# The sample's tile joins the last prompt batch in a fused attention and expert-retrieval kernel

## The reference

```python
h = rmsnorm(x, g_norm1); z = h @ w_in
x = x + concat[GLA(z_gla), FoX(z_fox)] @ w_out
h2 = rmsnorm(x, g_norm2)
q = (h2 @ w_q).reshape(blk, 8, 2, 128)
s = einsum('nhcd,hckd->nhck', q, subkeys)
s1, i1 = top_k(s[:, :, 0], 16); s2, i2 = top_k(s[:, :, 1], 16)
top, ti = top_k(s1[..., :, None] + s2[..., None, :], 16)
idx = i1[ti // 16] * 128 + i2[ti % 16]
coeff = softmax(top) * gelu(einsum('nhkd,nd->nhk', u_tab[idx], h2))
x = x + einsum('nhk,nhkd->nd', coeff, v_tab[idx])
```

## Time and profile before

| | |
|---|---|
| three runs | 3724.64, 3728.86, 3737.84 us, median 3728.86 |
| profiled execution | 3727.01 us, its span 3725.2 us |
| busy share of the span | PE 76%, DVE 71%, ACT 40%, POOL 35% |
| mean granted TensorE clock | 0.881 |
| gathers | 1056 issues; their queue moved 1131.10 MB |
| all DMA | 1268.10 MB, mean 340 GB/s |

### The profile page before, as it was taken

The page is one execution under the profiler, slowest core; times in us unless marked ns, Lnnn a source line. Parts: engine busy times, 40 slices in busy tenths (PEclk is TensorE's granted clock), DMA queues, the critical chain, the costliest instruction groups (busy, mean ns, idle before and its releaser), DMA issues.

```text
span 3725.2 us, 32330 instructions
## 1 busy us (share of the span) xinstructions
PE 2838.7 (76%) x8403; PEld 1468.9 (39%) x8403; DVE 2658.0 (71%) x5553; ACT 1479.7 (40%) x3869; POOL 1316.1 (35%) x1145
## 2 busy tenths in 40 slices
PE   7998998667777877677777677777877777687677
PEld 3454444543333343333334333333343333243333
DVE  5344334278688777899687798777777887887786
ACT  2333333135345633344543344444533443343344
POOL 0000000034444444444344434434444453444443
PEclk9999998788888888898889888878888898888889
DMA  4001000699999999999999999999999999999998
GB/s 190 23 23 46 23 23 22 263 360 417 411 417 399 419 419 419 375 403 402 415 420 420 420 407 419 355 400 400 420 420 419 413 411 406 410 404 414 420 418 350
DMA packets 187373, 1268.10 MB, mean 340 GB/s; under 512 B 23380, under 2 KB 24492, under 8 KB 39860
## 3 DMA queue, kind: packets, MB, share of 16 engines
q0 software_dynamic: 159488, 1131.10, 74.4%
q1 hardware_dynamic: 25348, 122.22, 8.2%
q10 hardware_dynamic: 2352, 12.72, 0.8%
HBM read 1239.08 MB, written 26.88 MB: 340 GB/s over the span
## 4 chain that ended last, share of the span: by engine, by line
DMA 33%; PE 21%; DVE 14%; issue 8%; ACT 4%; POOL 2%; SPq 0%; DVEq 0%; ACTq 0%; POOLq 0%
DMA uv_ring<-in_peer_uv,expert_index 32%; PE ps_acc L1458 14%; DVE uv_ring L1634 6%; PE ps_scores L1433 3%; DVE v_sums L1642 2%; POOL uv_ring L1098 2%; PE ps_scores L1314 1%; ACT coef_diag L1271 1%; PE ps_scores L1401 1%; ACT gelu_u_dot_h L1266 1%; DVE key_top_index L1544 1%; DVE key_scores_rest L1545 1%; PE ps_turn L1325 1%; DVE key_top_index L1553 1%; PE ps_fox_o L1332 1%
## 5 line engine op out<-in xcount | busy, mean ns | idle before, releaser
L1458 PE MATMUL ps_acc<-uv_ring,coef_diag 128*128 128x512 f32 x2676 | 1530.6, 714 | 743.2 <-ACT coef_diag L1271 725.8
L1098 POOL DMA_INDIRECT uv_ring<-in_peer_uv,expert_index x1056 | 1268.5, 1201 | 1661.8 <-PE ps_acc L1458 1467.8
L1634 DVE CUSTOM_DVE_ANT_0 uv_ring<-uv_ring,h_rows 128x1024 f32<-128x1024 f32 x1056 | 1286.5, 1221 | 460.0 <-DMA uv_ring<-in_peer_uv,expert_index 438.0
L1458 PEld LDWEIGHTS ps_acc<-uv_ring,coef_diag 128*128 128x128 f32 x2676 | 556.7, 222 | 1525.1 <-ACT coef_diag L1271 995.1
L1266 ACT ACTIVATE gelu_u_dot_h<-u_dot_h 128x2 f32<-128x2 f32 x528 | 107.1, 203 | 1317.1 <-DVE u_dot_h L1634 1315.2
L1642 DVE SCALAR_TENSOR_TENSOR v_sums<-uv_ring,coefficients,v_sums 128x1024 f32<-128x1024 f32 x387 | 496.2, 1282 | 10.5 <-ACT coefficients L1273 9.5
L392 PE MATMUL ps_z<-w_in,x_T 128*128 128x512 f32 x864 | 416.3, 630 | 5.7 <-DVE w_in L677 5.7
L1433 PE MATMUL ps_scores<-weight_chunk,rows_T 128*128 128x256 f32 x1152 | 261.9, 381 | 0.7 <-issue 0.7
L1271 ACT ACTIVATE coef_diag<-coef_diag,gelu_u_dot_h 128x128 f32<-128x128 f32 x669 | 253.1, 398 | 17.7
L1433 PEld LDWEIGHTS ps_scores<-weight_chunk,rows_T 128*128 128x128 f32 x1152 | 220.4, 192 | 62.5 <-issue 35.8
L392 PEld LDWEIGHTS ps_z<-w_in,x_T 128*128 128x128 f32 x864 | 164.8, 200 | 193.5 <-issue 181.3
(11 more groups left out here) (205 smaller groups left out, 2582.5 us busy)
## 6 DMA issues: line engine op xcount, KB each, us to landing
weight_chunk<-scratch_keys_w SPq DMA_DIRECT2D x48, 1024.0 KB
weight_chunk<-in_w_out_chunks SPq DMA_DIRECT2D x24, 1024.0 KB
uv_ring<-in_peer_uv,expert_index POOLq DMA_INDIRECT x1056
w_in<-in_w_in_chunks SPq DMA_DIRECT2D x6, 2048.0 KB, 25.4
uv_ring<-in_w_peer_q_T SPq DMA_DIRECT2D x8, 1024.0 KB, 24.9
x_T<-in_x_T POOLq DMA_DIRECT2D x9, 512.0 KB, 4.6
x_rows<-in_x_rows POOLq DMA_DIRECT2D x9, 512.0 KB, 5.3
x_mid<-in_x_rows SPq DMA_DIRECT2D x9, 512.0 KB, 15.9
```

Source lines behind the costliest of these rows:

```text
L1098: pool.indirect_dma_start(out=ring[:, s % RING, :], out_offset=None, in_=dram["uv"], in_offset=bass.IndirectOffsetOnAxis(ap=idx[:, t % IDX ...
L1458: mm = pe.matmul(acc[:, c, :], diag[:, r, :], ring[:, r, D + c * 512:D + (c + 1) * 512], start=first, stop=False, skip_group_check=True)
L1634: dve.tensor_tensor_reduce(out=ring[:, s % RING, 0:D], in0=ring[:, s % RING, 0:D], in1=h2[:, t % 2, :], scale=1.0, scalar=0.0, op0=ALU.mul ...
```

## The change

The sample's tile becomes the third of the last batch. Room for a third `x_mid` and `rows_T` comes from dropping both copies of `match_replace` (it now writes in place) and one buffer of `h2_rows`. With one buffer, h2 is remade at the first slot of a tile, after all dots of the tile before. Every second head of folded keys is staged in `k_pairs_T` in four pieces of 512 floats, and both stores name four pieces.

```diff
-BATCHES = [[0], [1], [2, 3], [4, 5], [6, 7], [8]]
+BATCHES = [[0], [1], [2, 3], [4, 5], [6, 7, 8]]
...
+def mix_free(t):
+    return (mix_fill(t) if PLACE[t + 2][0] == PLACE[t][0] else h2_fill(t)) + 2
...
-    s2 = sb("key_scores_rest", [P, 2, NKEY])
-    cand2 = sb("candidates_rest", [P, TOPK, TOPK])
-    h2 = sb("h2_rows", [P, 2, D])
+    h2 = sb("h2_rows", [P, D])
-    folded = [sums[:].rearrange("p b n -> p (b n)"), h2[:].rearrange("p b n -> p (b n)")]
+    folded = [sums[:].rearrange("p b (c n) -> p (b c) n", c=2), kT[:, :, P:P + 512]]
...
             if t >= 2:
-                sp.wait_ge(q_t, h2_fill(t - 2) + 2)
+                sp.wait_ge(q_t, mix_free(t - 2))
...
-                for n in range(2):
-                    pool.wait_ge(f_st[n], 16 * (PH // 2))
+                pool.wait_ge(f_st[0], 16 * (PH // 2))
...
-        act.wait_ge(init, 2)
+        act.wait_ge(init, 1)
...
+                    if t == 1:
+                        act.wait_ge(f_st[1], 16 * (PH // 2))
...
-            act.dma_start(dram["keys_w"][h], folded[h % 2]).then_inc(f_st[h % 2], 16)
+            act.dma_start(dram["keys_w"][h].rearrange("p (c n) -> p c n", c=4), folded[h % 2]).then_inc(f_st[h % 2], 16)
...
                     act.wait_ge(q_t, mix_fill(t) + 2)
+                    if i >= 2:
+                        act.wait_ge(q_t, h2_fill(t - 2) + 2)
...
-        dve.memset(cand2[:], 0.0).then_inc(init, 1)
...
-                        dve.wait_ge(q_t, h2_fill(t - 2) + 2)
+                        dve.wait_ge(q_t, mix_free(t - 2))
...
-                    did(dve.match_replace(out=rest(c), in_to_replace=v(c)[:, 0:8], in_values=values(c), imm_value=NEG_FILL))
+                    did(dve.match_replace(out=values(c), in_to_replace=v(c)[:, 0:8], in_values=values(c), imm_value=NEG_FILL))
...
-                if i == SLOTS - 4 and t < TILES:
-                    reopen(t + 1)
+                if i == 0 and 0 < t <= TILES:
+                    dve.wait_ge(dotted, SLOTS * t)
+                    reopen(t)
```

More of the change, by code:

```diff
@@ L1474, in fold_out @@
                 dve.wait_ge(f_st[h % 2], 16 * (h // 2))
-            dve.tensor_copy(folded[h % 2][:, part * 512:(part + 1) * 512], acc[:, u % 2, :]).then_inc(f_ev, 1)
+            dve.tensor_copy(folded[h % 2][:, part, :], acc[:, u % 2, :]).then_inc(f_ev, 1)
         def attend(t):
@@ L1535, in did, with top16 @@
                 return ins.then_inc(chain, 1)
-            def top16(values, rest, v, i, count):
+            def top16(values, v, i, count):
                 for c in range(count):
@@ L1548, in top16 @@
                 for c in range(count):
-                    did(dve.max(out=v(c)[:, 8:16], in_=rest(c)))
+                    did(dve.max(out=v(c)[:, 8:16], in_=values(c)))
                 yield
@@ L1552, in top16 @@
                 for c in range(count):
-                    ins = dve.max_index(out=i(c)[:, 8:16], in_max=v(c)[:, 8:16], in_values=rest(c))
+                    ins = dve.max_index(out=i(c)[:, 8:16], in_max=v(c)[:, 8:16], in_values=values(c))
                     if c < count - 1:
@@ L1560, in router @@
             wait(dve, kf_r, n)
-            ins = yield from top16(lambda c: keys[:, c, :], lambda c: s2[:, c, :], lambda c: kv[:, c, :], lambda c: ki[:, c, :], 2)
+            ins = yield from top16(lambda c: keys[:, c, :], lambda c: kv[:, c, :], lambda c: ki[:, c, :], 2)
             ins.then_inc(k_in, 1)
@@ L1570, in router @@
             flat = cand[:].rearrange("p a b -> p (a b)")
-            flat2 = cand2[:].rearrange("p a b -> p (a b)")
             wait(dve, tex, n)
-            ins = yield from top16(lambda c: flat, lambda c: flat2, lambda c: tv[:], lambda c: ti[:], 1)
+            ins = yield from top16(lambda c: flat, lambda c: tv[:], lambda c: ti[:], 1)
             ins.then_inc(top_r, 1)
@@ L1616, in reopen @@
             dve.wait_ge(p_rs, t + 1)
-            dve.scalar_tensor_tensor(out=h2[:, b, :], in0=sums[:, b, :], scalar=hrs[:, t:t + 1], in1=g2[:],
+            dve.scalar_tensor_tensor(out=h2[:], in0=sums[:, b, :], scalar=hrs[:, t:t + 1], in1=g2[:],
                                      op0=ALU.mult, op1=ALU.mult).then_inc(h_r, 1)
@@ L1633, in back @@
                         wait(dve, geld, g - 1)
-                    dve.tensor_tensor_reduce(out=ring[:, s % RING, 0:D], in0=ring[:, s % RING, 0:D], in1=h2[:, t % 2, :], scale=1.0, scalar=0.0,
+                    dve.tensor_tensor_reduce(out=ring[:, s % RING, 0:D], in0=ring[:, s % RING, 0:D], in1=h2[:], scale=1.0, scalar=0.0,
                                              op0=ALU.mult, op1=ALU.add, accum_out=dots[:, g % 2, n:n + 1]).then_inc(dotted, 1)
```

## The result

The changed kernel takes 3819.01 us (median of 4, 3814.15 to 3825.19) against 3730.5 in the same comparison: a ratio of 1.0232, 95% interval 1.0212 to 1.0252. It is slower, as forecast, but by 88 us where 27 were forecast, and outside the range of 3706 to 3802. Its profiled execution took 3817.34 us, its span is 3815.4.

A forecast was written before the change was run, and what follows sets the result against it. Transfers bound attention, projection and the last slots; VectorE's work plus its wait for scores bound routing of pairs. Terms summed to 3751 us of span, 3753 of time, plus 3 for waits: 3756, range 3706 to 3802.

The forecast's parts named there:

- Rival (a): Transfers bind in routing too, so fewer bytes win: 3712 us, or 3697 if only the bytes move; chance 0.25.
- Rival (b): At tile 8's attention TensorE waits for the past's keys and values, costing 10 to 30 us: 3775; chance 0.13.
- Rival (c): More badly placed routing units than counted, 7 us each, five more making 3790; chance inside the forecast's own 0.62.
- bad units: Routing units where VectorE waits about 8.3 us for key scores; 1, 2 and 2 counted in the last three batches.
- 3 us of margin: Added to the summed time because the wait for scores rises with VectorE's load, a third step up.
- Step 1: Start up to slot 0: 787 us, unchanged; stores in 2 KB pieces might cost 12 in all, taken as 0.
- 2, attention and projection: 446 slots where transfers bind, 507.1 MB at the old mean rate: 1223 us, denser work covered by idle engine time.
- Step 3: Routing of tile 0 in 110 us; of tile 1 in 153, 131 busy plus 22 idle as before.
- 4, pairs: Routing of tiles 2 and 3, and 4 and 5: 262 us busy, 26 and 33 waits, 5 idle: 293 and 300.
- 5, last batch: Routing of tiles 6, 7 and 8 up to slot 868: 356 us busy, 40 waits, 7 other: 403.
- 6, the rest: Last 187 slots, nearly pure transfers at 420 GB/s: 473 us, plus 9.4 from last dot to end: 482.
- The position: TensorE's step in ScalarE's copy slot behind adds, VectorE's one slot later, group ahead all TensorE's: 8.3 us wait.

The follow-up runs named there:

- shift of the steps: Changed kernel with VectorE's steps of a unit, and the ScalarE steps that follow, two front steps later: 3717.91 us; one front step later: 3760.49 us.
- density run: Kernel before, own batches and all 72 chunk loads, every due slot of the plan multiplied by 0.875: 3788.32 us, ratio 1.0153.
- old-batches run: Changed kernel with the old list of batches, so only its small edits and no shared pass: 3739.62 us, ratio 1.002.
- contiguous store: Changed kernel with every second head of folded keys staged in 8192 contiguous bytes of unused row buffers: 3814.85 us in a single execution.
- all repairs: Changed kernel with VectorE's steps two front steps later, folded keys in 8192-byte pieces and no adds on VectorE beside routing: 3689.59 us, ratio 0.989.

## Why the prediction was right in kind and wrong in size

Right: the kernel has two regimes; routing of pairs is set by VectorE and its wait for scores, not by transfers; the new plan makes all that precedes slot 868 denser and leaves the end to the transfers; the result is slower. The shift of the steps showed the wait and the density run the plan. Rival (a), transfers bind in routing, fell with both: VectorE waited 4.0 us for data in 311. Rival (b), the wait for the past, did not appear: in the stretch of the last attention TensorE waited for nothing but diagonals and probabilities. Rival (c), more bad units than counted, held for one unit, below.

The sum of 3751 us of span, before its 3 us of margin, was 64 short of 3815.4. By its own steps:

| step | forecast | measured |
|---|---|---|
| 1, up to slot 0 | 787 | 798.2 |
| 2, attention and projection | 1223 | 1226.9 |
| 3, routing of tile 0, of 1 | 110, 153 | 108.5, 161.6 |
| 4, pairs | 293, 300 | 310.8, 310.7 |
| 5, last batch | 403 | 413.2 |
| 6, the rest | 482 | 476.1 + 9.4 |

**Steps 3 to 5 failed by 46 us.** VectorE's time in them, split into its work, its wait for scores and its other idle time:

| stretch | forecast | measured |
|---|---|---|
| routing of 1 | 131 + 22 of idle | 131.0 + 22.0 + 8.6 |
| of 2 and 3 | 262 + 26 + 5 | 266.6 + 34.6 + 9.6 |
| of 4 and 5 | 262 + 33 + 5 | 266.6 + 32.4 + 11.7 |
| of the last batch | 356 + 40 + 7 | 358.7 + 43.0 + 11.5 |

The wait for scores is the largest part, some 25 us, and 14 of them stand where no unit was counted at all. Step 3 carried tile 1's idle time of before over, 22 us, of which 7.7 was wait for scores; the new plan made that wait 22.0. In the other three batches the wait was 11 us too low: the five units that the prediction counted (slots 242, 466, 478, 782, 794) waited 9.1, 7.9, 3.9, 8.9 and 4.1 us, not 8.3 each, one that it did not count waited 6.4 (slot 266), and all 49 uncounted ones had a mean of 1.6 and not 1.2. That the wait of tiles 4 and 5 came out right, 32.4 against 33, is luck: one of its two bad units was priced at twice its wait, and the others too low. VectorE's work was 12 us too low: a slot less took (285.0 - 266.6) / 14 = 1.31 us off its busy time with tiles 2 and 3, not 1.62, and why stays open. Other idle time was some 10 too low.

The position was defined too narrowly. Taken unit by unit from plan and trace, what matters is whether VectorE's step comes one slot after TensorE's or two. Before, 13 units stood one slot apart and waited 2.7 us each, 56 stood two apart and waited 0.7. The new plan puts 31 one slot apart, at 3.3 us, and 36 two apart, at 0.9. With tile 1 it is 6 of 8 units, where it was 3. With VectorE's steps one front step later only 6 units in all stand one slot apart, with two steps later none.

**Step 1 failed by 11 us**: the text bounded the stores in 2 KB pieces by 12 and took 0. The old-batches run put it at 8 for all small edits, the contiguous store at some 7 for the pieces.

**The range failed** since its upper end held the wait only as more units of 8 us and took the start as free. Besides, 0.25 of the chance lay on rival (a), whose own test, the 5 to 11 us of wait for data in the earlier trace rows, already spoke against it. The Trainium skill, Perfetto Trace Analysis, section Identifying the Most-Contended Engine, says to optimize the engine used most. Taken as the prediction took it for (a), that rule would have promised 3697 to 3712 here; the measured 3819 goes against it. The same page's section Optimization Strategy says that interleaving regimes may help, and the trace agrees: the last 187 slots, left nearly alone, had VectorE busy 62% beside full transfers, while routing from tile 1 to slot 868, packed denser, ran at only 363 to 382 GB/s.

## What to carry to other kernels

Where a static plan weaves two streams, loads saved in one place are paid in how dense the rest must be packed; price the packed stretch by its slowest engine plus its waits, not by bytes. A wait that is short at one density is long at the next: count the distance in slots between producer and consumer under the new plan, for every unit, before trusting a mean of the old one. Then ask the plan first: a heavier weight for the routing steps, one number, took back 94 us. And a repair of such a wait should be tried on the old kernel too: here two front steps made both the same, and only with VectorE freed of adds as well did the shared pass come out 19 us ahead.

## What was not expected of the hardware

The mean granted TensorE clock rose where TensorE got more to do: 0.87 in the routing of tiles 2 and 3 of the changed kernel (225 us busy of 311), 0.95 with the adds moved to it (249 of 296), 0.98 with all repairs (240 of 275). Its idle time there was 85.6, 46.9 and 34.4 us, and the 105 more matmuls of the first step cost only 24 us of busy time: the mean of one matmul of the adds fell from 727 to 635 ns. The unit near slot 242 shows the other side: after a stop of 6.75 us the clock was 0.50. The busy share alone does not tell the clock: in the run with the heavier weight, attention of tiles 2 and 3 had TensorE busy 108 of 129 us at a mean of 0.83.

Four stores of 1 MB read in rows of 2048 bytes from a tile with a stride had a median landing of 6.2 us, no worse than 7.7 before, but one took 15.9, and that one held the fold of a later head for 9.1 us. The old-batches run, which stages the same way, shows it too: its slowest took 14.5 us, and the fold waited 9.0.
